# Half of the third query columns loaded into other places, and a new order of places for the first U rows

## What is computed

```python
def block(xb):                       # 128 tokens at a time, two blocks
    q = (xb @ w_query).reshape(PEER_BLOCK, PEER_HEADS, 2, PEER_QDIM // 2)
    s = jnp.einsum('thpd,hpnd->thpn', q, sub_keys)
    sv, si = lax.top_k(s, PEER_TOPK)
    cand = (sv[:, :, 0, :, None] + sv[:, :, 1, None, :]).reshape(...)
    cidx = (si[:, :, 0, :, None] * N_KEYS + si[:, :, 1, None, :]).reshape(...)
    top_s, pos = lax.top_k(cand, PEER_TOPK)
    idx = jnp.take_along_axis(cidx, pos, axis=-1)
    gate = jax.nn.softmax(top_s.astype(jnp.float32), axis=-1)
    act = jax.nn.gelu(jnp.einsum('thkd,td->thk', expert_u[idx], xb).astype(jnp.float32))
    return jnp.einsum('thk,thkd->td', (gate * act).astype(xb.dtype), expert_v[idx])
```

## Time and profile before

| | us |
|---|---|
| median of 3 runs | 1857.94 (1857.42 to 1857.98) |
| profiled execution, its own time | 1859.15 |
| its span in the trace | 1857.4 |
| PE busy | 1594.0 (86%) |
| DVE busy | 1050.2 (57%) |
| ACT busy | 400.8 (22%) |
| POOL busy | 399.1 (21%) |
| bytes moved | 724.64 MB, mean 390 GB/s |

### The profile page before, as it was taken

One profiled execution on the slowest core, in us unless ns is written; L12 is line 12 of the kernel. 1 busy time (PEld: TensorE's weight loads), 2 busy tenths in 40 slices (PEclk: granted clock), 3 DMA queues, 4 the chain that ended last, 5 costly groups with the idle time before them and its releaser, 6 DMA issues. The chain is left out here.

```text
span 1857.4 us, 13296 instructions
## 1 busy us (share of the span) xinstructions
PE 1594.0 (86%) x4518; PEld 760.9 (41%) x4518; DVE 1050.2 (57%) x1706; ACT 400.8 (22%) x1168; POOL 399.1 (21%) x355
## 2 busy tenths in 40 slices
PE   6999999999999979999978786877759687687876
PEld 2445445565468854444323232332324233232332
DVE  2237875575568973433546556465565756646445
ACT  2121013232010032222212122121222212122112
POOL 0000000001004552345222121222213122121212
PEclk9999999999999989999999998989889899998998
DMA  9998877548969999999999999999999999999997
GB/s 401 427 375 342 323 285 265 220 186 358 420 250 372 417 421 427 425 427 427 429 428 427 429 428 427 427 428 428 429 428 408 428 427 429 428 429 427 428 428 299
DMA packets 69266, 724.64 MB, mean 390 GB/s; under 512 B 6968, under 2 KB 9352, under 8 KB 19536
## 3 DMA queue, kind: packets, MB, share of 16 engines
q0 software_dynamic: 49296, 613.75, 78.8%
q1 hardware_dynamic: 17264, 107.30, 14.2%
q10 hardware_dynamic: 2640, 2.75, 0.6%
HBM read 721.63 MB, written 2.15 MB: 390 GB/s over the span
## 5 line engine op out<-in xcount | busy, mean ns | idle before, releaser
L1359 PE MATMUL ps<-ring,wg 128*128 128x512 f32 x1056 | 500.6, 620 | 131.7 <-ACT wg L889 115.1
L1807 DVE SCALAR_TENSOR_TENSOR ring<-ring,A 128x2048 f32<-128x2048 f32 x144 | 329.5, 2292 | 315.2 <-DMA ring<-in_expert_rows,acc 309.0
L1359 PEld LDWEIGHTS ps<-ring,wg 128*128 128x128 f32 x1056 | 202.0, 197 | 421.5 <-issue 245.8
L883 ACT ACTIVATE rows_and_values<-rows_and_values 128x1 f32<-128x1 f32 x256 | 51.3, 200 | 845.9 <-DVE ring L1807 488.6
L542 POOL DMA_INDIRECT ring<-in_expert_rows,acc x126 | 144.9, 1150 | 404.7 <-PE ps L1359 391.4
L1063 PE MATMUL ps<-ring,H 128*128 128x512 f32 x512 | 222.0, 593 | 0.0
L1359 PE MATMUL ps<-rows_and_values,wg 128*128 128x512 f32 x336 | 155.2, 605 | 29.1 <-ACT wg L889 27.4
L1386 DVE SCALAR_TENSOR_TENSOR ring<-ring,rows_and_values 128x2048 f32<-128x2048 f32 x64 | 143.7, 2288 | 48.1 <-DMA ring<-in_mod_late 35.6
L1359 PE MATMUL ps<-H,wg 128*128 128x512 f32 x264 | 124.1, 615 | 34.7 <-ACT wg L889 34.7
L1359 PE MATMUL ps<-queries_and_gates,wg 128*128 128x512 f32 x256 | 119.1, 609 | 32.8 <-ACT wg L889 32.8
L1063 PEld LDWEIGHTS ps<-ring,H 128*128 128x128 f32 x512 | 96.4, 190 | 119.5 <-issue 119.2
(11 more groups left out here) (290 smaller groups left out, 1473.8 us busy)
## 6 DMA issues: line engine op xcount, KB each, us to landing
ring<-in_mod_late POOLq DMA_DIRECT2D x32, 2048.0 KB, 10.2
ring<-in_mod_first SPq DMA_DIRECT2D x16, 2048.0 KB, 20.1
ring<-in_w_in SPq DMA_DIRECT2D x14, 2048.0 KB, 11.5
ring<-in_w_query SPq DMA_DIRECT2D x7, 2048.0 KB, 14.4
ring<-in_w_out SPq DMA_DIRECT2D x12, 1024.0 KB, 10.1
H<-in_tokens SPq DMA_DIRECT2D x4, 1024.0 KB, 12.8
queries_and_gates<-in_w_in SPq DMA_DIRECT2D x2, 1024.0 KB, 22.8
queries_and_gates<-neg_rows ACTq DMA_DIRECT2D x8, 256.0 KB, 5.6
```

The lines of the kernel that those rows point to most:

```text
L883: link(nc_a.activation(act_t[:, r:r + 1], dots[:, r:r + 1], ACT.Gelu_apprx_tanh))
L1359: ins = mm(ps[:, 4 * b + n, :], diag[:, place % 4, :], row[:, n * CH:(n + 1) * CH], start=k == 0, stop=r == BLOCK_RANKS - 1, skip_group_ch ...
L1807: v.scalar_tensor_tensor(out=rows_u, in0=rows_u, scalar=1.0, in1=A[:, r // BLOCK_RANKS, :], op0=ALU.mult, op1=ALU.mult, accum_out=dots[:, ...
```

## The change

Three things are changed.

1. Half `kh` = 0 of the third query columns is loaded by SP into `gy` and the first row of `VXf` (in `rows_and_values`), not into `W[2]`. Its first 1 MiB waits for `y_ready`, its second for `h2_ready` at 4, and both stand one step earlier in SP's list, right behind the two loads of n = 1.
2. Since `gy` and `VXf` (places 7 and 4) are now taken until PE has read them (`w_free` 46), the U rows have other places: the three tables are changed as the diff shows, and so are POOL's waits on `w_free`. `LATE_SLOTS` is not changed.
3. ACT's copy of scores into `H` waits for the last rank in place 9 or 10, which for place 9 is now rank 4.

```diff
-EARLY_SLOTS = (4, 7, 9, 10, 2, 3) + (4, 7, 2, 3) * 3 + (4, 7)
-MIDDLE_SLOTS = (8, 6, 2, 3, 4, 7, 0, 1)
+EARLY_SLOTS = (9, 10, 2, 3, 9, 0, 1) + (2, 3, 0, 1) * 3 + (2,)
+MIDDLE_SLOTS = (8, 6, 3, 0, 1, 2, 4, 7)
 LATE_SLOTS = (6, 2, 3, 4, 0, 1, 5)
...
-        WQ2 = {1: [KT[:], fours(gwork)], 0: [W[2][:, 0:4], W[2][:, 4:8]]}
+        WQ2 = {1: [KT[:], fours(gwork)], 0: [fours(gy[:]), fours(VXf[:, 0:D])]}
...
             for n in range(1, 4):
+                if n == 2:
+                    sp.wait_ge(S["y_ready"], 1)
+                    load_third_query(0, 0, q_ld[0])
+                    sp.wait_ge(S["h2_ready"], 2 * TB)
+                    load_third_query(0, 1, q_ld[0])
+                    continue
                 for i, kh in enumerate(HALVES):
-                    if n == 2 and kh == 1:
-                        continue
                     sp.wait_ge(S["w_free"], 36 + 2 * n + i + 1)
                     load_query(n, kh)
...
                 if r == EARLY_SLOTS.index(2):
                     pool.wait_ge(S["w_free"], 41)
+                if r == EARLY_SLOTS.index(0):
+                    pool.wait_ge(S["w_free"], 42)
                 if r == len(EARLY_SLOTS):
                     pool.wait_ge(S["w_free"], 45)
-                if r == len(EARLY_SLOTS) + MIDDLE_SLOTS.index(0):
+                if r == len(EARLY_SLOTS) + MIDDLE_SLOTS.index(4):
                     pool.wait_ge(S["w_free"], 46)
                 gather_u(r)
...
-                    act.wait_ge(S["u_free"], EARLY_SLOTS.index(9 + b) + 1)
+                    act.wait_ge(S["u_free"], max(r for r in range(LEAD) if u_slot(r) == 9 + b) + 1)
...
-                        pe.wait_ge(q_ld[kh], 32)
+                        pe.wait_ge(q_ld[kh], 48)
```

## The result

| | before | after |
|---|---|---|
| median of 5 runs | 1857.42 us (1856.89 to 1857.98) | 1877.49 us (1876.93 to 1878.12) |
| profiled execution: own time, span | 1859.15, 1857.4 | 1877.49, 1875.8 |

The ratio is 1.0108, with a 95% interval of 1.0097 to 1.0119: the changed kernel is slower by 1.1%. The median rose by 20.1 us; the two profiled executions lie 1877.49 - 1859.15 = 18.3 us apart.

A forecast was written before the change was run, and what follows sets the result against it. DMA bytes were taken to bound the kernel from some 572 us on. Holding rank 37 for dot 33 delays the first V matmul 18.7 us; 1857.9 + 18.6 gave 1876.5 us, range 1872.5 to 1880.

The forecast's parts named there:

- the sum: Delay of PE's first V matmul, worked out from dot 33 onward: 18.7 us, added to the median as 18.6.
- What bounds it: From some 572 us on, DMA bytes set the end; idle DMA time added or removed earlier moves it equally.
- Part 1, the load: 2 MiB of SP loads moved into the DMA hole near 550, delaying no gather; worth at most 4.9 us.
- Part 2, the first ranks: Early U gathers wait for PE and dots, giving back 4 to 5 us; net 0.3 to 2.5 us gained by 592.
- Part 3, rank 37: POOL holds rank 37 and all V gathers for dot 33, draining the DMA queue; first V matmul 18.7 us later.
- V row 0: Last term before PE's first V matmul: one 1.049 MB row behind row 37 at 427 GB/s, 2.46 us.
- check by bytes: Second way to the delay: V row 0 starts moving near 692.3 instead of 674.3, 18.0 us later; agreement within 0.7.
- The rule against the row: Rank 37's issue beside a dot: trace row's 2.75 us taken over the skill's bare issue, which would give 16.9 total.
- (a): Rank 37 not held or queue not drained; the end moves only 0.3 to 2.5 us, 4.9 at most; chance 0.07.
- (b): PE takes over: longer idle keeps its clock low, delaying V gathers 7 and 8; 3 to 6 us more; chance 0.07.
- (c): Part of the delay given back, by a 0.94 us issue and the loss at 1380: 14.6 us; chance 0.10 under 1874.

The follow-up runs named there:

- kernel 1: The changed kernel with rank 37 in place 3 (last used by rank 30) instead of place 2; 1856.51 us against 1857.55, ratio 0.9997.
- 6: kernel 1 without its two moved 1 MiB loads of the third query columns; 1856.49 us, ratio 0.9998.
- 5: The kernel before without the 2 MiB load of the third query columns' half kh = 0; 1856.76 us against 1857.5, ratio 0.9998.
- kernel 8: kernel 1 with another early order: rank 7 in place 10 instead of place 2; 1857.9 us, ratio 1.0003.
- kernel 2: The kernel before with only rank 37 moved, to place 7 (last used by rank 33), so held for dot 33; 1877.8 us, ratio 1.0108.
- kernel 4: The changed kernel with rank 37 in place 7 (last used by rank 35), held two dots longer; median 1880.74 us.
- kernel 9: The changed kernel moving only one MiB early, with reordered places, rank 37 in place 2 (last used by rank 31); 1856.89 us against 1857.64, ratio 0.9996.

## Why the prediction was right

The forecast of 1876.5 (1872.5 to 1880) met 1877.49, and by the mechanism that it named. That it came within 1.0 us is in part luck: the median rose by 20.1 us where the sum had 18.6, and 0.5 of the difference is hidden because the median of before came out at 1857.42 and not at the 1857.94 that the sum was added to.

- **What bounds it.** Bytes carry the delay to the end: from kernel 1 to after, the first V matmul moves by 20.7 us, the last matmuls by 21.0, the median by 21.0. Nothing behind gave any of it back.
- **Part 1, the load.** Both 1 MiB loads ran at 541.74 and 549.42, and are free there (6). "Worth at most 4.9 us" was a bound; the worth was 0.7 us, within what a run can tell (5). The step missed that the old load filled a gap: the gap was seen only when the load was taken out. The expectations for 5 missed it as well, by both theories.
- **Part 2, the first ranks.** Rank 2 was issued at 566.58 as worked out, after 4.41 us of waiting for PE, and the forecast net of 0.3 to 2.5 us by 592 compares with 1.4 by bytes. One of its causes was wrong: rank 7 was not held for dot 2 (see kernel 8); the gap near 578 comes from the long issues beside dots. That this part would not enter the sum, since DVE's chain hangs on PE's last scores, held too.
- **Part 3, rank 37.** Shown by 1 and 2 from both sides. Step by step: dot 33 done 685.64 (forecast 686.07), issue at 686.00 (686.42), its length 2.75 (2.75), row 37 at its reader 4.83 us after the issue's end (4.67). The one mis-sized term is **V row 0, "one row behind, 2.46 us"**: its reader starts at 697.10, 3.52 us after the reader of row 37 at 693.58. Windows from the one start to the other, in after, in kernel 4 and in kernel 2:
```profile
693.58:697.10 3.52, 0.00 (x1) 0.03 (x1) 2.30 (x2) 0.00 (x0) 2.91 (x3) 0.50 1.01 377
697.79:701.30 3.51, 0.00 (x1) 0.03 (x1) 2.30 (x2) 0.00 (x0) 2.90 (x3) 0.50 1.01 427
693.32:696.33 3.01, 0.00 (x0) 0.03 (x1) 2.30 (x2) 0.00 (x0) 2.87 (x1) 0.50 1.01 408
```
  In after 3.52 x 377 kB = 1.33 MB, not one row of 1.05, flowed between the two starts, as if DMA engines done with row 37 had gone on to later rows: 0.65 us at 427 GB/s. And these bytes flowed at 377 GB/s, which costs the other 0.4 us. In kernel 4 it is 1.50 MB at 427, in kernel 2 1.23 MB at 408 and only 3.01 us. So more than one row flowed each time. That the engines had run on to later rows is argued from these bytes, not shown engine by engine. Why the rate was low in after stays open: kernel 2 had 408 GB/s with V rows 0 and 1 issued in 1.91 us each too. The step of the forecast's check by bytes that has V row 0 start moving near 692.3 shows no working, so its agreement within 0.7 proves little.
  The first V matmul is then 18.7 - 0.4 (dot 33 was done at 685.64, not 686.07) + 0.2 (row 37 at its reader) + 1.1 (V row 0) = 19.5 us later, with rounding what the trace has.
- **The rule against the row.** The issue beside a running dot took 2.75 us and the following ones 1.91; without a dot it took 0.94. The row was right. The Trainium skill (SBUF — State Buffer, Who interferes with whom) says that `tensor_tensor`, which has no two-port mode, was not seen to stall GpSimd's descriptor generation; taken to the dot and to this issue, it would have given the bare issue and 16.9 in all. For this pair, a `scalar_tensor_tensor` with two SBUF inputs beside an indirect gather, which reads its row numbers from SBUF (`acc` in the rows), the trace disagrees with that.
- **The median.** The sum was to be 18.7 against the profiled execution; by own times it is 18.3. The first V matmul gave 0.8 more than the sum, and a slow stretch of the profile of before (412 GB/s from 1380 to 1440; after has 421 from 1400 to 1460) takes 1.3 us off again. The median rose 1.7 more than the profiled time, since the profiled execution of before was itself 1.7 us above its median: the kernels 1, 5 and 6, whose medians lie 0.7 to 1.0 us under before's, start V at 676.4 to 676.7, before's profile at 677.64. Only one execution of before has a trace, so whether its first V matmul stood earlier in the others is not shown.
- **Rivals.** (a) fell: the queue drained. (b) fell: the granted clock stayed at 0.50 until 700 and was 0.91 in the next window, but the first 32 passes took 15.77 us (17.04 before), and V gathers 7 and 8 waited 2.42 and 2.49 us for PE, which cost no bytes (424 GB/s at 700). In kernel 4 a longer idle time added nothing. (c), part given back, did not come true: the issue took 2.75 us and not 0.94, and the slow stretch of the profile of before at 1380 is no gift of the delay, since kernel 1, which has no idle stretch, is faster there too (419 GB/s).

## What to carry to other kernels

Where one engine issues transfers in a fixed order, look at the last few before each change of stage: a buffer place that is freed by work behind a reduction or a softmax holds everything queued behind it. In a DMA-bound kernel such a hole is paid in full at the end (21 us here), while bytes moved forward ahead of it can be lost again in it (0.8 of the 1.0 MB of kernel 9). After a table of places is rewritten, work out for every reuse which consumer frees the place, and where that consumer stands in its engine's order; exchanging two entries was worth 21 us here. And before a transfer is moved into a gap, take it out once: the move alone can't be expected to gain more than the time falls by, and here that was 0.7 us.

## What the runs showed of the hardware

- An indirect gather's issue on POOL takes 0.94 us with no dot running, and 1.91 us back to back beside dots of 2.2 us on 128x2048 f32 from SBUF. What sets the length is the end of the dot: a first issue beside a dot runs from 686.00 to 688.75 (2.75 us), 0.89 us past the end of the dot that had started at 685.64. In the twelve traces of this case, between 550 and 760 us, all 341 gather issues that start 0.05 us or more into a dot end 0.87 to 0.96 us after that dot's end (2.21 us after its start, where the next dot can begin), and so take up to 3.06 us; one that started 0.02 us into a dot (594.61 in before) took 0.94. At 1.91 us of issue and 0.30 between two, a row of 1.049 MB can be asked for every 2.21 us, barely faster than the 2.46 us in which it is moved.
- Behind an emptied queue the rate is uneven: 193, 377 and 387 GB/s in three windows of 4 us before the 424 of the next (after), 207, 416, 381 and 346 in kernel 2. With short issues (kernel 4) it was 418 in the second two-microsecond window behind the first data, and 412 and 430 from 696 to 704.
- After 28 us without a matmul, PE ran at a granted clock of 0.50 for some 3.5 us, from 697.10 on, and had 1.00 from 702 on. After 8.72 us without one, in before, it started at 677.64 and the window 680 to 684 still shows 0.52. So the longer idle time of 28.46 us cost no more low-clock time than the shorter one did.
